# Spreading the first layer's attention gate rows with four selector products instead of transfers through memory

## The chip, the cores and the metric

The kernel runs on one NeuronCore of a Trainium2 chip. The metric is the device time of one launch in microseconds (us). Engines are named as the profile names them: PE (TensorE, matrix products), DVE (VectorE), ACT (ScalarE), POOL (GpSimd), SP (SyncE, which here only issues transfers). SBUF is the memory beside the engines, with 128 partitions; PSUM is the small memory that PE writes, eight banks of 128 x 512 float32.

## What is computed

Two token groups of 128 tokens each (t = 0, the prompt; t = 1, the sample) pass through two layers. Every layer has an attention part and a mixture-of-experts part, each with a residual that is scaled by a gate:

```python
for l in range(DEPTH):                      # 2 layers, D_MODEL = 1024
    sh, sc, g, shf, scf, gf = _modulation(cond, w_mod[l], b_mod[l])   # each 1 x 1024, per token group
    h = _adaln(x, norm_mix[l], sh, sc)      # rmsnorm(x) * (1 + scale) + shift
    o = attention(h) @ w_out                # 128 x 1024
    x = x + g * o                           # g is the same row for all 128 tokens of a group
    x = x + gf * _moe(_adaln(x, norm_ffn[l], shf, scf), w_router, ..., w_gate[l], w_up[l], w_down[l])
```

All is float32. The attention gate `g` is one row of 1024 numbers per token group. Tokens lie on the partitions, so to multiply `o` (128 tokens x 1024) by `g`, that row must stand on all 128 partitions.

## The kernel before

**Stages.** For each layer the kernel runs the input projection, the attention, the output projection, the second normalisation and the router, and then the experts. The 16 experts are taken in eight pairs; each pair streams 24 MB of weights through a ring of six slots of 2 MB (`ring`), plus some places in `work`, `gbuf`, `tmp`, `early`, `m4` and `spare` for the first pair. SP issues every weight load in a fixed order, and each load into a slot first waits for PE to have read what stood there.

**Order by hand.** During attention each engine follows a table, `FILL`. Attention has eight turns (four head batches for t = 1, then four for t = 0). In turn j, PE transposes the probabilities (`probs_transposed`, records at L799), computes the scores of turn j + 2 (L906), does what `FILL[l][(j,)]` lists, multiplies by the values (L938 or L944), and does what `FILL[l][j]` lists. The names in the table: `mod` is a quarter of the modulation product (L821), `modT` and `nextT` its transposition (L832), `wo` a half of the output projection (L868, eight products), `oT` the transposition of some outputs, `rt` router logits, `pos` token positions. ACT and DVE follow the same table for their own shares.

**Banks.** Every such PSUM result is a named job. The list `psum_jobs()` numbers them; job k is written to bank 1 + (k + 5) mod 7, and PE waits for job k - 7 to have been emptied (`bank_free`). Bank 0 is apart: it takes the modulation sums, and `keep_busy` writes there dummy 128 x 128 products (L845). When the experts of a layer begin, PE waits first for that one of the last seven jobs that lies on bank 1 (`before[0]`), since the first expert product writes banks 0 and 1; then it runs `keep_busy` (two of them in layer 0, three in layer 1) and then `gather`, whose first eight products (L1048) wait for DVE's one-hot table `picked`. The other six (`behind`) are waited for one product later.

**The gate rows.** The modulation leaves each gate as a pair of 512-wide rows in a few partitions of the tile `gates`; all its other rows but the experts' gates are zero. After DVE has added the bias (`gates_taken`), POOL runs `spread_gates(l)`: two transfers write the rows to `gate_rows` in memory (L734), then, once these have landed, two transfers read each token group's row back onto all 128 partitions of `gbuf` (L740, 512 KB each). DVE's `out_project` waits for `gate_spread[t]` and multiplies the projection's bank by `gbuf` (L1688), then adds to `x` (L1690). The experts' gates take another way already: `expert_gate_rows` multiplies `gates` by a column of the constant `selg`, repeated 128 times, so that each of four products puts one half row on all partitions of a bank (L1122), and ACT copies the banks to `gbuf` (L1418).

Of the kernel before, what the change touches and what calls it, by code (L numbers as in the profile page):

```python
# [8 lines left out]
ACT = mybir.ActivationFunctionType  # L9
# [4 lines left out]
P = 128  # L14
# [88 lines left out]
def turn(l, j):  # L103
# [10 lines left out]
        1: [("T", 0), ("mod", 0, 2, 2), ("mod", 0, 2, 3)],  # L114
        2: [("modT", 2), ("mod", 1, 0, 0), ("mod", 1, 0, 1)],
        3: [("mod", 1, 0, 2), ("oT", 1), ("mod", 1, 0, 3)],
        4: [("wo", 0, 1), ("nextT", 0)],
        5: [("wo", 1, 1)],
        (6,): [("mod", 1, 1, 0)],
        6: [("oT", 0)],  # L120
# [19 lines left out]
def banks_of(l, item):  # L140

    kind, rest = item[0], item[1:]
    if kind == "mod":
        return []
    if kind == "in":
        return [("qkv", l) + rest]
    if kind == "nextT":
        return [("modT", 1) + rest]
    if kind == "T":
        return [("T", l, rest[0], i) for i in range(2 + K_JOBS[l, rest[0]])]  # L150
    if kind == "hT":
        return [("hT", l) + rest + (h,) for h in range(2)]
    if kind == "xT":
        return [("xT", l, h) for h in range(2)]
    if kind == "hk":
        return [("hk", l, rest[0], h) for h in range(2)]
    if kind == "rt":
        return [("rt", l, rest[0])] + (banks_of(l, ("hk", 1)) if rest[0] else [])
    if kind == "pos":
        return [("pos", l), ("count", l)]  # L160
    return [(kind, l) + rest]
# [16 lines left out]
def released(l):  # L178

    order = [("mod", 0, 0, k) for k in range(4)] if l == 0 else []  # L180
    for point in points(l):
        for item in FILL[l].get(point, []):
            if item[0] == "mod":
                order.append(item)
            elif item[0] in ("in", "wo") and item[2] == 0:
# [2 lines left out]


EMPTIED_BY = {"vecT": "dve", "bT": "dve", "modT": "dve", "T": "act", "S": "act", "PT": "act",  # L190
              "O": "dve", "oT": "act", "wo": "dve", "hk": "act", "rc": "dve", "pos": "dve", "count": "dve"}


APART = ("in", 0, 4)
# [59 lines left out]
def build(nc, a):  # L254
    ctx = ExitStack()
    with ctx:
# [11 lines left out]
        hT = sb("hT", [P, DC, TT * P])  # L268
        work = sb("work", [P, 15360])
        const = sb("const", [P, NCONST])  # L270
        gates = sb("gates", [P, LAYERS, UC])
        gbuf = sb("gbuf", [P, 4, UC])
# [13 lines left out]
        rc = sb("rc", [P, NE])  # L286
# [28 lines left out]
        def K(name):  # L315
            at, n = CONST[name]
            return const[:, at:at + n]
# [45 lines left out]
        def htok(t):  # L363
# [7 lines left out]
        filled = sem("bank_filled")  # L371
        emptied = {"act": sem("bank_emptied_act"), "dve": sem("bank_emptied_dve")}
# [18 lines left out]
        gate_spread = [sem(f"gate_spread{t}") for t in range(TT)]  # L391
        gates_out = sem("gates_out")
        gate_rows = nc.dram_tensor("gate_rows", (LAYERS, TT, D), F32, kind="Internal").ap()
        copies, bias_copied = nc.dram_tensor("bias_copies", (16, 3, 64, 32), F32, kind="Internal").ap(), sem("bias_copied")
        mod_used, mod_emptied, mod_ready, gates_taken = (
            sem(n) for n in ("mod_used", "mod_emptied", "mod_ready", "gates_taken"))
# [81 lines left out]
        def fill(name):  # L478

            return number[name] + 1  # L480
# [17 lines left out]
        def emptied_by(name):  # L498

            return emptied[engine_of[name]], done_at[name]  # L500
# [5 lines left out]
        def bank_of(name):  # L506
            return bank[1 + (number[name] + SHIFT) % 7]
# [183 lines left out]
        def _(pool):  # L691
# [38 lines left out]
            def spread_gates(l):  # L730

                pool.wait_ge(gates_taken, 2 * l + 1)
                for u in range(2):
                    pool.dma_start(gate_rows[l, :, UC * u:UC * (u + 1)], gates[32 * u:32 * u + 2, l, :]).then_inc(gates_out, 16)  # L734
                if l == 1:
                    pool.wait_ge(x_ready, 8)
                    pool.wait_ge(filled, fill(("S", 1) + turn(1, BATCHES - 1) + (1,)))
                pool.wait_ge(gates_out, 32 * (l + 1))
                for t in (1, 0):
                    pool.dma_start(gbuf[:, 2 * t:2 * t + 2, :].rearrange("p u n -> p (u n)"),  # L740
                                   gate_rows[l, t].partition_broadcast(P)).then_inc(gate_spread[t], 16)

            for l in range(LAYERS):
                if l == 1:
                    power("norm", 1, 0, 1)
                    power("norm", 1, 0, 0)
                    pool.wait_ge(filled, fill(("qkv", 1, 1, 1)))
                    pool.dma_start(cache[:, 0:1024], a["cache_c_k"][0, 0].rearrange("k h d -> k (h d)")).then_inc(ld_cache[1], 16)
                    pool.dma_start(cache[:, 1024:2048], a["cache_c_v"][0, 0].rearrange("k h d -> k (h d)")).then_inc(ld_cache[1], 16)
                    pool.wait_ge(bias_copied, 48)  # L750
                    for r in range(2):
                        for r2 in range(2):
                            src = bass.AP(copies.tensor, copies.offset + (r2 - r + 1) * 64 * 32 + 15, [[31, 64], [3 * 64 * 32, 16], [1, 64]])
                            pool.dma_start(bias[64 * r:64 * r + 64, :, 64 * r2:64 * r2 + 64], src).then_inc(ld_bias, 16)
                power("qk", l, 1)
                power("qk", l, 0)

                pool.wait_ge(normed, 2 * l + 2)
                pool.wait_ge(*emptied_by(("qkv", l, IN_UNITS[l] - 1, 0)))
                if l == 0:  # L760
                    outs = [("new_a_k", 512, 128), ("new_a_v", 640, 128), ("new_b_k", 1280, 512), ("new_b_v", 1792, 512)]
                else:
                    outs = [("new_c_k", 1024, 1024), ("new_c_v", 2048, 1024)]
                for name, at, n in outs:
                    pool.dma_start(a[name], qkv[0][:, at:at + n]).then_inc(out_kv[l], 16)
                if l == 0:
                    power("sub", 0, 1)
                spread_gates(l)
                if l == 0:
                    power("sub", 0, 0)  # L770
                power("norm", l, 1, 1)
                power("norm", l, 1, 0)
# [5 lines left out]
        def _(pe):  # L778
# [82 lines left out]
            def out_project(l, u, t):  # L861
                w = ring[arrived(("out", l, u))]
                b = bank_free(("wo", l, u, t))
                pe.wait_ge(*emptied_by(("O", l, t, ORDER[l][-1])))
                if l == 0:
                    pe.wait_ge(*emptied_by(("oT", 0, t)))
                for c in range(DC):
                    ins = pe.matmul(b[:, :], oT(l, t, c), w[:, c, :], start=c == 0, stop=c == DC - 1)  # L868
                ins.then_inc(filled, 1)

            def outputs_transposed(l, t):
                pe.wait_ge(o_ready, 2 - t)
# [133 lines left out]

            def meanwhile(l, point):
                job = {"in": project, "modT": mod_transposed, "wo": out_project, "rt": logits, "hk": token_rows,
                       "oT": outputs_transposed, "hT": norm, "T": heads_transposed, "pos": positions}
                for item in FILL[l].get(point, []):  # L1010
                    if item[0] == "mod":
                        mod(*item[1:])
                    elif item[0] == "nextT":
                        mod_transposed(1, item[1])
                    elif item[0] in ("rc", "xT"):
                        {"rc": shift_logits, "xT": rows_transposed}[item[0]](l)
                    else:
                        job[item[0]](l, *item[1:])
# [207 lines left out]
        def _(act):  # L1226
# [116 lines left out]
            def probs_transposed(l, j):  # L1343
# [3 lines left out]
                for k in range(pt_jobs(l, t, b)):  # L1347
# [3 lines left out]
                                   bank_of(name)[:, 0:per * P].rearrange("p (c q) -> p c q", c=per),  # L1351
                                   ACT.Copy).then_inc(emptied["act"], 1)

            def outputs_transposed(l, t):
                act.wait_ge(filled, fill(("oT", 0, t)))
                act.activation(oT(0, t, 4, 4), bank_of(("oT", 0, t))[:, :], ACT.Copy).then_inc(emptied["act"], 1)

            def meanwhile(l, point):
                for item in FILL[l].get(point, []):
                    if item[0] == "in" and engine_of[("qkv", l) + item[1:]] == "act" or item[0] == "in" and squared_cols(l, item[1]):  # L1360
                        project(l, *item[1:])
                    elif item[0] == "mod" and item[3] == 3:
                        mod(*item[1:3])
                    elif item[0] in ("oT", "hT") or item[0] == "T" and l == 1:
                        {"oT": outputs_transposed, "hT": modulate, "T": heads_transposed}[item[0]](l, *item[1:])

            def attention(l):
                meanwhile(l, "head")
# [94 lines left out]
        def _(dve):  # L1463
# [219 lines left out]
            def out_project(l, u, t):  # L1683

                name, k, cols = ("wo", l, u, t), 2 * t + u, slice(u * UC, (u + 1) * UC)
                dve.wait_ge(gate_spread[t], 16 * (l + 1))
                dve.wait_ge(filled, fill(name))
                dve.tensor_tensor(tmp[:, k % 2, :], bank_of(name)[:, :], gbuf[:, k, :], ALU.mult).then_inc(emptied["dve"], 1)  # L1688
                dve.wait_ge(*emptied_by(name))
                dve.tensor_tensor(x[:, t, cols], x[:, t, cols], tmp[:, k % 2, :], ALU.add).then_inc(x_ready, 1)  # L1690
# [307 lines left out]
```

## Time and profile before

| | us |
|---|---|
| three runs | 1262.09, 1263.69, 1263.94 |
| median | 1263.69 |
| the profiled execution, own time | 1262.51 |
| its span | 1260.70 |
| PE busy (matmul) | 1175.7 (93%) |
| DVE busy | 280.3 (22%) |
| ACT busy | 186.8 (15%) |
| POOL busy | 56.3 (4%) |
| memory traffic | 494 MB, 392 GB/s over the span |

A busy time is the sum of the intervals in which an engine had an instruction in work. The share of the 16 DMA engines says how much of a stretch they were moving data. The profile also gives the chain of work that ended last, which goes from the last instruction back to whatever released each step. A float32 product appears in it as two records.

The main stages by time in the span: attention of layer 0 to about 190 us, its experts to 643, attention of layer 1 to about 808, its experts to the end.

### The profile page before, as it was taken

The page shows a single profiled execution, that of the slowest core. Times are in us where ns is not written, and L with a number is a line of the kernel's source. Part 1 is how long each engine was busy: PE and PEld are TensorE (multiplying, and loading weights), DVE is VectorE, ACT ScalarE, POOL GpSimd, SP SyncE. Part 2 cuts the span into 40 slices and gives each one's busy share as a digit, 9 for nine tenths or more (in the row PEclk, how much of TensorE's full clock was granted, in tenths as well). Part 3 has the DMA queues.
Part 4 walks back from the last instruction along what each step waited for, and adds up shares of the span by engine and source line. Part 5 has one row for each costly group of instructions (what it writes and reads, how often), then busy time and mean ns, then how long its engine had stood idle before and what let it go on. Part 6 is the DMA issues. An engine that isn't in the chain of part 4 may idle for free.

```text
span 1260.7 us, 13886 instructions
## 1 busy us (share of the span) xinstructions
PE 1175.7 (93%) x5521; PEld 515.2 (41%) x5521; DVE 280.3 (22%) x677; ACT 186.8 (15%) x439; POOL 56.3 (4%) x68
## 2 busy tenths in 40 slices
PE   4999999999998899898999999999999899889998
PEld 2445454443433243333344455643434334343433
DVE  1146532122010102020233353312020111102013
ACT  1224321010000000000122342210000001000010
POOL 0422000000000000000003020000000000000000
PEclk9999999999989999999999999999999999998999
DMA  9999999999999999999994678699999999999997
GB/s 374 392 378 353 414 421 428 423 400 410 426 430 427 429 427 429 428 428 429 418 389 126 221 285 347 281 405 402 371 427 431 425 432 425 432 425 432 424 425 303
DMA packets 60223, 494.07 MB, mean 392 GB/s; under 512 B 5506, under 2 KB 6674, under 8 KB 28948
## 3 DMA queue, kind: packets, MB, share of 16 engines
q1 hardware_dynamic: 57136, 485.85, 93.1%
q0 software_dynamic: 2864, 7.46, 2.0%
q8 instruction: 29, 0.48, 0.2%
q10 hardware_dynamic: 180, 0.17, 0.0%
q14 instruction: 14, 0.11, 0.0%
HBM read 490.69 MB, written 3.16 MB: 392 GB/s over the span
## 4 chain that ended last, share of the span: by engine, by line
PE 74%; DMA 20%; issue 3%; ACT 1%; DVE 1%; SPq 1%; POOL 0%; DVEq 0%
PE bank L1087 40%; DMA ring<-in_w_gate 13%; PE bank L858 12%; PE bank L868 4%; PE bank L1057 3%; DMA ring<-in_w_up 3%; PE bank L821 3%; PE bank L1048 2%; PE bank L1109 2%; DMA ring<-in_w_in_ab 2%; PE bank L799 2%; DMA ring<-in_w_down 1%; PE bank L906 1%; PE bank L1139 1%; PE bank L1122 1%
## 5 line engine op out<-in xcount | busy, mean ns | idle before, releaser
L1087 PE MATMUL bank<-ring,hT 128*64 128x512 f32 x2688 | 610.7, 610 | 60.0 <-issue 27.5
L1087 PEld LDWEIGHTS bank<-ring,hT 128*64 128x64 f32 x2688 | 204.7, 140 | 443.4 <-issue 441.9
L858 PE MATMUL bank<-ring,hT 128*128 128x512 f32 x320 | 143.0, 605 | 2.5 <-DMA ring<-in_w_in_ab 2.4
L858 PEld LDWEIGHTS bank<-ring,hT 128*128 128x128 f32 x320 | 60.9, 193 | 80.0 <-issue 77.4
L1848 DVE TENSOR_TENSOR work<-work,bank 128x512 f32<-128x512 f32 x56 | 38.5, 687 | 195.1 <-PE bank L1057 194.9
L1841 DVE TENSOR_TENSOR work<-work,bank 128x512 f32<-128x512 f32 x32 | 22.0, 688 | 229.0 <-PE bank L1087 198.0
L1048 PE MATMUL bank<-work 128*128 128x128 f32 x512 | 60.5, 276 | 0.2 <-DVE work L1822 0.2
L1048 PEld LDWEIGHTS bank<-work 128*128 128x128 f32 x512 | 58.7, 192 | 2.1 <-issue 1.6
L868 PE MATMUL bank<-ring,work 128*128 128x512 f32 x128 | 56.5, 594 | 0.3 <-DVE work L1665 0.3
L1398 ACT ACTIVATE hT<-bank 128x512 f32<-128x512 f32 x32 | 19.0, 595 | 255.2 <-PE bank L1139 255.2
L1889 DVE COPY work<-bank 128x512 f32<-128x512 f32 x14 | 9.7, 692 | 209.3 <-PE bank L1087 209.3
L1057 PE MATMUL bank<-work 128*128 128x512 f32 x112 | 51.8, 605 | 0.0
L821 PE MATMUL bank<-ring,cond 128*32 128x512 f32 x384 | 48.3, 629 | 1.5 <-DMA ring<-in_w_mod 1.0
L1109 PE MATMUL bank<-ring,hT 128*64 128x512 f32 x192 | 42.2, 593 | 0.3 <-DMA ring<-in_w_down 0.3
L1829 DVE TENSOR_TENSOR work<-work,bank 128x512 f32<-128x512 f32 x32 | 22.0, 688 | 84.7 <-ACT work L1407 84.7
L1087 PE MATMUL bank<-work,hT 128*64 128x512 f32 x152 | 39.3, 593 | 0.0
L1425 ACT ACTIVATE work<-bank 128x512 f32<-128x512 f32 x14 | 8.4, 597 | 192.9 <-PE bank L1087 192.9
L868 PEld LDWEIGHTS bank<-ring,work 128*128 128x128 f32 x128 | 23.7, 190 | 27.6 <-issue 27.6
L1411 ACT ACTIVATE work<-bank 128x256 f32<-128x256 f32 x16 | 6.1, 383 | 184.3 <-PE bank L1162 184.3
L1407 ACT ACTIVATE work<-bank 128x512 f32<-128x512 f32 x32 | 19.1, 597 | 95.2 <-PE bank L1087 95.2
L1057 PEld LDWEIGHTS bank<-work 128*128 128x128 f32 x112 | 20.1, 189 | 31.5 <-issue 31.5
L1562 DVE TENSOR_REDUCE hss<-bank 128x8 f32<-128x512 f32 (+1 forms) x16 | 10.5, 658 | 91.7 <-ACT bank L1298 91.7
(213 smaller groups left out, 718.6 us busy)
## 6 DMA issues: line engine op xcount, KB each, us to landing
ring<-in_w_gate SPq DMA_DIRECT2D x64, 2048.0 KB, 16.8
ring<-in_w_up SPq DMA_DIRECT2D x52, 2048.0 KB, 17.2
ring<-in_w_down SPq DMA_DIRECT2D x52, 2048.0 KB, 16.9
ring<-in_w_mod SPq DMA_DIRECT2D x23, 2048.0 KB, 10.2
work<-in_w_up SPq DMA_DIRECT2D x8, 2048.0 KB, 16.6
ring<-in_w_down SPq DMA_DIRECT2D x12, 1024.0 KB, 14.7
ring<-in_w_in_c SPq DMA_DIRECT2D x6, 2048.0 KB, 20.8
ring<-in_w_in_ab SPq DMA_DIRECT2D x4, 2048.0 KB, 21.6
```

The source lines that it names most:

```text
L799: ins = pe.transpose(b[:, i * P:(i + 1) * P], src, K("ident"))
L821: ins = pe.matmul(out, cond[:, 2 * k + r, :], cols, start=(k, r) == (0, 0), stop=(k, r) == (3, 1), tile_position=(0, 32 * j))
L858: ins = pe.matmul(b[:, 0:n], hT[:, c, t * P:(t + 1) * P], w[:, c, 0:n], start=c == 0, stop=c == DC - 1)
L868: ins = pe.matmul(b[:, :], oT(l, t, c), w[:, c, :], start=c == 0, stop=c == DC - 1)
L1048: ins = pe.matmul(bank[2 if first and h else h][:, c * P:(c + 1) * P], htok(t)[:, at:at + P], pick[:, t, :], start=t == 0, stop=t == 1)
L1057: pe.matmul(bank[4 + 2 * t + h][:, :], GT[:, t, :], yd[:, h * UC:(h + 1) * UC], start=True, stop=True).then_inc(m["scattered"], 1)
L1087: ins = pe.matmul(bank[banks[j]][64 * e:64 * e + 64, :], lhs[:, 4 * h + c, 64 * e:64 * e + 64], weights(e, c, j), start=(h, c) == (0, 0), ...
L1109: ins = pe.matmul(bank[banks[j]][64 * e:64 * e + 64, :], lhs[:, 4 * h + c, 64 * e:64 * e + 64], rows4[slots[e]][:, c, j * UC:(j + 1) * UC] ...
L1407: act.activation(sg[:, h * UC:(h + 1) * UC], bank[h][:, :], ACT.Sigmoid).then_inc(m["sig_done"], 1)
L1829: dve.tensor_tensor(hid[:, half], sg[:, half], bank[h][:, :], ALU.mult).then_inc(m["gate_taken"], 1)
L1841: dve.tensor_tensor(hid[:, half], hid[:, half], bank[2 + h][:, :], ALU.mult).then_inc(m["hid_done"], 1)
L1848: dve.tensor_tensor(y[:, t, cols], y[:, t, cols], bank[4 + 2 * t + h][:, :], ALU.add).then_inc(m["y_added"], 1)
```

## The change

In layer 0 the gate rows no longer go through memory. Two entries come into the table, `gs` for t = 1 in turn 4 and for t = 0 in turn 5, each between the scores and the values. For each, PE runs two products of a repeated `selg` column with `gates`, and ACT copies the two banks to `gbuf`. DVE's `out_project` waits for these copies. POOL calls `spread_gates` only in layer 1. Layer 1 keeps its transfers.

```diff
+        (4,): [("gs", 1)],
         4: [("wo", 0, 1), ("nextT", 0)],
+        (5,): [("gs", 0)],
         5: [("wo", 1, 1)],
...
+    if kind == "gs":
+        return [("gs", l, rest[0], u) for u in range(2)]
...
-                pool.wait_ge(gates_out, 32 * (l + 1))
+                pool.wait_ge(gates_out, 32)
...
-                spread_gates(l)
+                if l == 1:
+                    spread_gates(l)
...
+            def gates_spread(l, t):
+
+                pe.wait_ge(gates_taken, 2 * l + 1)
+                for u in range(2):
+                    b = bank_free(("gs", l, t, u))
+                    i = 2 * u + t
+                    pe.matmul(b[:, :], K("selg")[:, i:i + 1].to_broadcast([P, P]), gates[:, l, :], start=True, stop=True).then_inc(filled, 1)
...
+            def gates_spread(l, t):
+                for u in range(2):
+                    name = ("gs", l, t, u)
+                    act.wait_ge(filled, fill(name))
+                    act.activation(gbuf[:, 2 * t + u, :], bank_of(name)[:, :], ACT.Copy).then_inc(emptied["act"], 1)
...
-                dve.wait_ge(gate_spread[t], 16 * (l + 1))
+                dve.wait_ge(*(emptied_by(("gs", 0, t, u)) if l == 0 else (gate_spread[t], 16)))
```

PE's instructions in turn 4 of layer 0, before (scores at L906, values at L938, the output projection at L868, then the transposition of the next layer's modulation at L832):

```order
L906 MATMUL bank3<-work 128x128
L938 MATMUL bank4<-work 128x128 [waits bank_emptied_act]
L938 MATMUL bank4<-work 128x128
L868 MATMUL bank5<-ring5,work 128x512 [waits bank_emptied_dve,bank_emptied_act,dense_loaded5]
L868 MATMUL bank5<-ring5,work 128x512 x7
L832 MATMUL bank6<-const,m4 128x128 [waits bank_emptied_dve,mod_emptied]
```

and after, where the same statements have the line numbers 919, 951, 873 and 837:

```order
L919 MATMUL bank3<-work 128x128
L882 MATMUL bank4<-gates,const 128x512 [waits bank_emptied_act,gates_taken]
L882 MATMUL bank5<-gates,const 128x512 [waits bank_emptied_act]
L951 MATMUL bank6<-work 128x128 [waits bank_emptied_act,bank_emptied_dve]
L951 MATMUL bank6<-work 128x128
L873 MATMUL bank7<-ring5,work 128x512 [waits bank_emptied_dve,bank_emptied_act,dense_loaded5]
L873 MATMUL bank7<-ring5,work 128x512 x7
L837 MATMUL bank1<-const,m4 128x128 [waits bank_emptied_act,mod_emptied]
```

Two products now stand between the scores and the values, and the jobs behind them lie two banks further on. Turn 5 has the same form and moves what follows by two banks more.

Four jobs more in the list also move every later job by four banks. At the start of layer 1's experts PE has before (token counts at L1004 and L1005, three `keep_busy` products at L845, the first gathering at L1048):

```order
L1004 MATMUL bank4<-chosen,const 128x16 [waits bank_emptied_dve]
L1005 MATMUL bank4<-chosen,const 128x16
L845 MATMUL bank0<-const 128x128 [waits bank_emptied_act]
L845 MATMUL bank0<-const 128x128 x2
L1048 MATMUL bank0<-work 128x128 [waits picked1]
```

and after (L1017, L1018, L850, L1061):

```order
L1017 MATMUL bank1<-chosen,const 128x16 [waits bank_emptied_dve]
L1018 MATMUL bank1<-chosen,const 128x16
L850 MATMUL bank0<-const 128x128 [waits bank_emptied_act,bank_emptied_dve]
L850 MATMUL bank0<-const 128x128 x2
L1061 MATMUL bank0<-work 128x128 [waits picked1]
```

The token counts (job `count`) now lie on bank 1, so `before[0]` is this job, and the wait ahead of the `keep_busy` products takes in DVE's reading of it. In layer 0 the job on bank 1 is now `pos` (token positions) in place of a job of ACT.

## Rows read from the trace of the kernel before

**Rows 1.** The page: busy us, then tenths busy in 40 equal slices.

```profile
PE 1175.7 (93%) x5521; PEld 515.2 (41%) x5521; DVE 280.3 (22%) x677; ACT 186.8 (15%) x439; POOL 56.3 (4%) x68
...
DMA  9999999999999999999994678699999999999997
```

**Rows 2.** The chain that ended last, layer 0: start, length, what (us).

```profile
140.00 6.87 PE bank L868 x16
...
281.59 20.75 PE bank L1087 x96
...
330.19 21.14 DMA ring<-in_w_gate
```

**Rows 3.** Who PE waited for, 113 to 320 us (all rows): total, times, longest.

```profile
PE bank L1087 <- ACT hT L1393: 1.3, 2, 0.8
PE bank L1000 <- issue: 0.6, 1, 0.6
PE bank L799 <- ACT hT L1266: 0.5, 1, 0.5
PE bank L944 <- ACT work L1350: 0.4, 2, 0.2
```

**Rows 4.** Windows: length, busy of PE, PEld, DVE, ACT, POOL, then PEclk, DMA share, GB/s.

```profile
137.00:149.00 12.00, 11.98 (x61) 6.34 (x54) 3.17 (x11) 2.82 (x12) 0.00 (x0) 1.00 1.02 423
276.00:278.00 2.00, 2.00 (x14) 1.21 (x11) 0.69 (x1) 0.42 (x1) 0.00 (x0) 1.00 0.46 197
290.00:292.00 2.00, 2.00 (x12) 0.70 (x10) 0.00 (x0) 0.00 (x0) 0.00 (x0) 1.00 0.72 279
292.00:640.00 348.00, 318.74 (x1449) 124.94 (x1446) 51.43 (x104) 28.03 (x50) 0.00 (x0) 0.97 1.01 427
```

**Rows 5.** What SP's transfer queue waited for, 270 to 300 us.

```profile
SPq L557 <- PE bank L1087: 27.3, 3, 12.8
```

**Rows 6.** The chain: the four selector products that spread the experts' gates.

```profile
606.02 3.63 PE bank L1122 x8
```

**Rows 7.** ACT's timeline: its next instruction after turn 4's exponentials, and one gate copy.

```profile
147.59 0.38 ACT L1350 ACTIVATE work<-bank 128x256 f32<-128x256 f32 x1 [5.70 <-PE bank L799]
...
607.12 0.60 ACT L1418 ACTIVATE gbuf<-bank 128x512 f32<-128x512 f32 x1 [0.42 <-PE bank L1122]
```

**Rows 8.** Transfers of 130 to 147 us: POOL's queue, then what it carried.

```profile
q0 software_dynamic: 288, 1.05, 15.4%
gbuf<-gate_rows POOLq DMA_DIRECT2D x2, 512.0 KB, 8.1
```

**Rows 9.** DVE's first use of a gate row in layer 0.

```profile
146.98 0.69 DVE L1688 TENSOR_TENSOR tmp<-bank,gbuf 128x512 f32<-128x512 f32 x1 [6.30 <-PE bank L868]
```

**Rows 10.** Timeline at the start of layer 1's experts.

```profile
807.65 0.92 PE L845 MATMUL bank<-const 128*128 128x128 f32 x6
...
808.59 0.17 DVE L1786 TENSOR_REDUCE cnt<-bank 128x1 f32<-128x16 f32 x1
...
808.73 2.05 PE L1048 MATMUL bank<-work 128*128 128x128 f32 x16 [0.17 <-DVE work L1822]
```

**Rows 11.** Five `keep_busy` products without a wait, layer 1, PE's timeline.

```profile
802.57 1.28 PE L845 MATMUL bank<-const 128*128 128x128 f32 x10
```

**Rows 12.** Windows of layer 1, columns as in rows 4.

```profile
810.00:812.00 2.00, 1.22 (x10) 0.82 (x10) 0.62 (x4) 0.60 (x1) 0.00 (x0) 1.00 0.04 14
892.00:894.00 2.00, 2.00 (x17) 1.76 (x16) 0.69 (x1) 0.60 (x1) 0.00 (x0) 1.00 0.61 131
896.00:1240.00 344.00, 315.69 (x1442) 124.45 (x1442) 46.41 (x97) 29.11 (x52) 0.00 (x0) 0.97 1.00 425
```

**Rows 13.** The chain: 32 records of one expert product at full and at lower clock.

```profile
429.88 7.09 PE bank L1087 x32
...
469.01 8.78 PE bank L1087 x32
```

## What the change does to the time, forecast before it ran

> **What bounds the kernel now.** The page comes first: PE is busy 93% of the span, and the DMA engines show a 9 in 34 of 40 slices [rows 1]. Both look like the bound, so busy shares decide nothing here, and the stage has to be asked. The change acts on layer 0 between 118 and 165 us.
>
> The chain of waits is the second view. Through turns 4 and 5 it runs on PE from one product to the next, and it stays with it (the experts' products at 281.59 us) until 330 us, where it first passes to a weight load of the experts' loop [rows 2]. The third view says how far PE can give way: from 113 to 320 us PE waits 2.8 us in all (1.3 + 0.6 + 0.5 + 0.4), never for a transfer, and each of these waits hangs on ACT or DVE work, or on issue, that itself follows PE's own earlier results [rows 3]. In turn 4 PE is busy 11.98 of 12.00 us at full clock [rows 4]. So an instruction more on PE here has no gap to go into.
>
> That alone doesn't carry a delay to the end, since the memory also streams at 423 GB/s in the same stretch [rows 4]: if transfers set the pace, PE's delay would be swallowed. Here the windows are read for places where the DMA engines run dry. Between 276 and 278 us their share falls to 0.46, and between 290 and 292 to 0.72; from 292 to 640 us it is full, at 427 GB/s [rows 4]. What was missing in the gaps was permission: SP's queue spent 27.3 of these 30 us waiting for PE to free a ring slot [rows 5]. A DMA system that has run dry keeps no memory of work saved earlier; what it does next starts when PE lets it. So up to about 290 us layer 0 is paced by PE, and from there by transfers. The last handing over, at about 290 us, takes place as late as PE is late, and the 350 us behind it only shift. Layer 1 has the same form: the DMA engines are at 0.04 at 810 us and at 0.61 at 892 us, and full only behind that [rows 12].
>
> **The four products.** The twin of the added product runs already for the experts' gates: four products of a repeated column with `gates`, 3.63 us on the chain, 0.91 each [rows 6]. The added ones have the same operands, shapes and count. Their waits are met: `gates_taken` is raised by DVE in turn 0, and the banks they take were emptied by ACT or DVE a turn earlier. Split into two visits they cost +3.6 us on PE. As bounds: an output projection's eight products take 6.87 us, 0.86 each, with pipelining between neighbours [rows 2], which gives 3.4; one wasted gap a visit, of the size of the longest wait in rows 3 (0.8), gives 5.2. I take 3.6, since that row is the same instruction. None of it is covered, by the 11.98 of 12.00 us.
>
> The TensorE page of the Trainium skill ("TensorE: Matmul & The Clock Gate", section "Back-to-back issue gap") gives N/2.4 + 2.5 ns for an isolated matmul of N columns, 216 ns for 512. Four products would then be 0.9 us. The trace disagrees for these float32 products, at 0.91 us for one; the measurement decides.
>
> **ACT's copies.** Four copies of a 128x512 bank at 0.60 us each are 2.4 us [rows 7]. ACT does a pair behind the exponentials of turns 4 and 5. After turn 4's exponentials it idles 5.70 us until the next transposition is there [rows 7], so 1.2 us fit. In turn 5 the pair stands likewise ahead of a wait for PE's next 7 us projection. Cost 0. Were the cover gone, PE would wait for ACT to copy probabilities: up to 1.2 us a turn.
>
> **DVE's wait.** `out_project` waits for ACT's copy instead of the transfer. DVE's first use of a gate row now waits 6.30 us for the projection on PE, not for the gates [rows 9], and the copies will be done at about 143.1 us (147.59 - 5.70 + 1.2), against a projection that ends at 146.98 + 1.8 = 148.8. Behind that wait stand the residual add and the shares of turn 5; none of them moves by more than PE does. Cost 0, gain 0.
>
> **The transfers.** 1.05 MB leave POOL's queue; they took 15.4% of 16 engines over 17 us, which is 2.6 us of the whole DMA system, and landed after 8.1 us [rows 8]. The weight loads behind them may land up to 2.6 us sooner. No one waited for them up to 320 us [rows 3], and at 276 us the engines run dry whatever was saved [rows 4]. Gain 0 on the path. As a bound on the gain: 2.6 us, if transfers carried the pace after all. POOL also loses a wait for the landing of the first pair; POOL is busy 4% and its next work is asked for by DVE much later. Nothing.
>
> **The banks.** Four more jobs move every later bank by four of seven. Which job waits for which (k - 7) is the same except near the new jobs, where the job waited for is at least most of a turn old. What does change is `before[0]`, on which PE waits ahead of `keep_busy`. In layer 0 it becomes `pos`, read by DVE before PE has finished the next modulation transposition: 0. In layer 1 it becomes `count`. DVE reads the count only after its first one-hot table, from 808.59 to 808.76 us [rows 10]. PE before did its three dummy products from 807.65 us while that table was made, and began to gather at 808.73 [rows 10]. Now the dummies begin only at about 808.76 plus the 0.05 us with which PE followed DVE's table, so 808.81, and only behind them the gathering. Five such products take 1.28 us as ten records of 275 ns that overlap: (1.28 - 0.28) / 9 = 0.11 between records, 0.22 per product [rows 11]; three are 0.67 us. Gathering starts at 809.48, +0.75 us. The bounds are 0 (if the dummies slip through at once) and 0.08 + 0.92 = 1.0 (the whole interval of rows 10). The DMA engines are all but dry at 810 to 812 us [rows 12], and the next loads wait for the product behind this gathering, so these 0.75 us pass to the end too.
>
> **Sum.** 3.6 + 0.75 = 4.35 us. Against the profiled execution that is 1262.5 + 4.35 = 1266.9 (span 1260.7 to 1265.1). The profiled execution lies 1.2 under the median of the runs, and the same difference on the median gives 1263.7 + 4.35 = 1268.0.
>
> **Rivals.**
> (a) *Transfers carry the pace, and the 1.05 MB saved are worth their time.* The delay of PE in layer 0 is then swallowed by loads that have landed ahead of their use, and 2.6 us are gained; layer 1's 0.75 stays: 1263.7 - 2.6 + 0.75 = 1261.9. For it: the DMA share is full in turn 4 [rows 4], and the chain ends on weight loads in both loops. Against it: the dry gaps at 276 and 290 us. It decides if in the changed kernel no dry gap stands between 206 and 300 us; the gap now is 0.54 of 2 us, 1.1 us, at 276 to 278 and it should widen. This is the case that is not slower. The Trainium skill's "Perfetto Trace Analysis", section "Identifying the Most-Contended Engine", says to rank engines over the profile by occupancy or memory use and optimise the first; by that, with the memory close to its rate nearly throughout, less traffic should win. The trace speaks against it in this stretch.
> (b) *Part of the delay is taken back.* PE's waits of rows 3 shrink because DVE, ACT and POOL go on while PE is with the new products. At most 2 us of the 2.8 could go: 1266.0. Against it: they all hang on PE results that come later by the same amount.
> (c) *The clock falls in layer 1.* PE's idle time around 808 to 811 us rises from 0.95 us (0.17 in rows 10 and 0.78 in rows 12) to 1.7 with the dummies displaced. At the lower of the two clocks, 1.2 GHz, a stretch of 32 records took 8.78 us in place of 7.09 [rows 13], so +1.7: 1269.7. For it: the loop does lose its clock after waits of PE. Against: in rows 12 the clock stays 1.00 with 0.78 us idle in two.
> (d) *ACT or a bank delays PE in turn 4 or 5*: up to 1.2 us a turn, 1268.0 + 1.2 = 1269.2 for one.
> (e) *The displaced dummies cost nothing*: 1263.7 + 3.6 = 1267.3.
>
> **How the numbers follow.** The forecast, 1268.0, with 0.60; (a) 0.08; (b) 0.10; (c) 0.08; (d) 0.06; (e) 0.08. A measurement of this kernel can tell about 0.2%, 2.5 us, from no change. Faster by more needs under 1261.2: only (a) with a lucky spread of runs, 0.03. Within 0.2% (to 1266.2): the rest of (a), most of (b), and a tail of the forecast in runs that scatter by 1 us to either side, 0.19. Slower: 0.78. The range leaves out (a) and the far end of (c) and of (d): 1264.9 to 1270.4, where the bounds of the costs (3.4 + 0 to 5.2 + 1.0) span 1267.1 to 1269.9, and the rest is the scatter of runs and (b).
>
> **What would show it.** Right: four products of 0.9 us at two places near 140 and 150 us, no wait of PE ahead of them; PE's first record behind turn 5 late by 3.6; the dry gap that was at 276 us later by 3.6 and wider, by up to 2.6 us more; layer 1 entered 3.6 late; its dummies after DVE's count, and 0.7 to 0.8 us more by the first expert product. Wrong: weight loads of the second expert pair that start earlier relative to the span's start than before (a); a wait of PE for ACT at the values of turns 4 to 6 (d); a granted clock under 1 near 812 us (c). The forecast as a whole falls if the experts of layer 0 end less than 2 us later than before.

## The result, and the profile of the changed kernel

| | us | against before |
|---|---|---|
| before, median of 4 runs | 1263.82 (1262.09 to 1265.32) | |
| changed, median of 4 runs | 1272.12 (1271.78 to 1273.33) | ratio 1.0068, 95% interval 1.0050 to 1.0085 |
| profiled execution, before and changed | 1262.51 and 1271.78 | span 1260.7 and 1270.0 |

The changed kernel is slower by 8.3 us, where 4.35 had been forecast, and outside the forecast range of 1264.9 to 1270.4. The direction held. The place and the size of the first term, the four products, held too. The second term, 0.75 us for a wait that moved in layer 1, is where it went wrong.

The chain of waits, in order of time (start, length, what), first in layer 0; of the kernel before, beside [rows 2]:

```profile
156.15 1.85 PE bank L821 x16
...
644.50 0.88 PE bank L799 x8
```

and of the changed kernel:

```profile
138.68 1.91 PE bank L882 x4
141.04 6.87 PE bank L873 x16
149.24 1.91 PE bank L882 x4
151.60 6.87 PE bank L873 x16
158.90 1.85 PE bank L826 x16
...
647.49 0.88 PE bank L804 x8
```

The product behind turn 5 (now L826) starts at 158.90, where before it started at 156.15. But this execution ran 0.61 us ahead when it came to turn 4. PE's timeline has its scores there, before and changed:

```profile
138.58 0.71 PE L906 MATMUL bank<-work 64*128 64x128 f32 x8
137.97 0.71 PE L919 MATMUL bank<-work 64*128 64x128 f32 x8
```

That difference is scatter: in two experiments below whose code is that of the kernel before up to here, the same scores began at 137.90 and 136.98. From the scores to the product behind turn 5 it took 158.90 - 137.97 = 20.93 us, before 156.15 - 138.58 = 17.57, so the two visits cost 3.36 us. Layer 1 is entered at 647.49 in place of 644.50, which is 2.99 later, or 3.6 with the 0.61. That part is as forecast.

PE's waits from 113 to 320 us in the changed kernel are those of [rows 3] again:

```profile
PE bank L1100 <- ACT hT L1412: 1.3, 2, 0.8
PE bank L1013 <- issue: 0.6, 1, 0.6
PE bank L804 <- ACT hT L1279: 0.5, 1, 0.5
PE bank L957 <- ACT work L1363: 0.4, 2, 0.2
```

None shrank, and none was added. Now the start of layer 1's experts, PE's timeline, which answers to [rows 10]; the first line is of the kernel before, its first expert product, and the others are of the changed kernel:

```profile
811.56 7.09 PE L1087 MATMUL bank<-ring,hT 128*64 128x512 f32 x32 [0.78 <-ACT hT L1393]
...
810.41 0.37 PE L1018 MATMUL bank<-chosen,const 128*128 128x16 f32 x2
812.03 1.62 PE L850 MATMUL bank<-const 128*128 128x128 f32 x6 [1.25 <-DVE cnt L1805]
813.45 3.62 PE L1061 MATMUL bank<-work 128*128 128x128 f32 x16
817.85 8.92 PE L1100 MATMUL bank<-ring,hT 128*64 128x512 f32 x32 [0.78 <-ACT hT L1412]
```

and the windows of the same stretch (length; busy of PE, PEld, DVE, ACT, POOL; then PEclk, DMA share, GB/s), which answer to [rows 12]:

```profile
808.00:810.00 2.00, 1.61 (x13) 1.43 (x13) 1.73 (x11) 1.34 (x3) 0.00 (x0) 1.00 0.94 401
810.00:812.00 2.00, 0.78 (x7) 0.68 (x7) 1.71 (x14) 0.00 (x0) 0.00 (x0) 0.84 0.96 381
812.00:814.00 2.00, 1.97 (x9) 2.00 (x10) 1.56 (x8) 0.00 (x0) 0.00 (x0) 0.50 0.28 108
...
818.00:820.00 2.00, 2.00 (x6) 0.67 (x7) 0.00 (x0) 0.00 (x0) 0.00 (x0) 0.50 0.00 0
820.00:822.00 2.00, 2.00 (x8) 0.66 (x6) 0.00 (x0) 0.00 (x0) 0.00 (x0) 0.60 0.00 0
822.00:824.00 2.00, 2.00 (x12) 0.64 (x10) 0.00 (x0) 0.00 (x0) 0.00 (x0) 1.00 0.03 8
```

PE stands idle for 1.25 us, waiting for DVE to read the token counts (L1805). While it does, the granted clock falls to half, 1.2 GHz, and it is back only in the window of 820 to 822 us. At half clock the three dummy products, the gathering and a part of the first expert product run. The pieces are measured from PE's router logits, which stand on both chains (L966 before, L979 changed) and come 2.98 us later:

```profile
799.55 1.83 PE bank L966 x16
802.53 1.83 PE bank L979 x16
```

| | before | changed | more |
|---|---|---|---|
| start of gathering | 808.73 | 813.45 | 4.72 - 2.98 = 1.74 |
| gathering and ACT's copy | 2.83 | 4.40 | 1.57 |
| first expert product to its end | 7.09 | 8.92 | 1.83 |
| sum | | | 5.14 |

Of the first 1.74 us, 0.75 is what the forecast had, 0.24 is that PE followed DVE's reading of the counts later than forecast, and the other 0.75 is that the three dummies took 1.42 us to the start of gathering in place of 0.67. So about 1.0 us of the 5.14 is waiting, and about 4.15 us is work at the lower clock.

What follows only shifts: the first gap of issue in the experts' loop comes 8.12 us later.

```profile
935.53 2.15 issue
943.65 2.00 issue
```

The spans differ by 9.3 us since in this one execution the clock also fell once in the last pair (the chain has 8.78 us at 1210.29, before 7.09 at 1202.21). The medians differ by 8.3.

### The profile page after: what moved, and what is told of

The parts are those of the page before. It is cut to its first block, busy times and chain, and to the rows that moved or that the text cites. A ratio compares the mean times of both kernels' runs of the same rounds, so it can differ in the third digit from the quotient of the medians.

```text
span 1270.0 us, 13904 instructions
## 1 busy us (share of the span) xinstructions
PE 1179.2 (93%) x5529; PEld 518.0 (41%) x5529; DVE 280.3 (22%) x677; ACT 188.9 (15%) x443; POOL 54.2 (4%) x64
## 4 chain that ended last, share of the span: by engine, by line
PE 73%; DMA 20%; issue 3%; SPq 2%; DVE 1%; ACT 1%; POOL 0%; DVEq 0%
PE bank L1100 40%; DMA ring<-in_w_gate 10%; PE bank L863 9%; DMA ring<-in_w_up 7%; PE bank L873 4%; PE bank L1122 3%; DMA ring<-in_w_mod 3%; PE bank L1061 3%; PE bank L1070 3%; PE bank L826 3%; PE bank L804 2%; PE bank L1152 1%; PE bank L919 1%; SPq L547 1%; PE bank L1135 1%
## 5 line engine op out<-in xcount | busy, mean ns | idle before, releaser
L863 PE MATMUL bank<-ring,hT 128*128 128x512 f32 x320 | 140.3, 595 | 2.5 <-DMA ring<-in_w_in_ab 2.4
L1061 PE MATMUL bank<-work 128*128 128x128 f32 x512 | 62.1, 280 | 0.0
L1061 PEld LDWEIGHTS bank<-work 128*128 128x128 f32 x512 | 60.4, 197 | 1.7 <-issue 1.6
L826 PE MATMUL bank<-ring,cond 128*32 128x512 f32 x384 | 48.0, 625 | 3.3 <-DMA ring<-in_w_mod 2.8
L1352 ACT ACTIVATE work<-bank,nm 128x256 f32<-128x256 f32 (+1 forms) x64 | 26.0, 421 | 31.4 <-DVE nm L1657 31.4
```

Of the source, the lines that this page charges most:

```text
L826: ins = pe.matmul(out, cond[:, 2 * k + r, :], cols, start=(k, r) == (0, 0), stop=(k, r) == (3, 1), tile_position=(0, 32 * j))
L863: ins = pe.matmul(b[:, 0:n], hT[:, c, t * P:(t + 1) * P], w[:, c, 0:n], start=c == 0, stop=c == DC - 1)
L1061: ins = pe.matmul(bank[2 if first and h else h][:, c * P:(c + 1) * P], htok(t)[:, at:at + P], pick[:, t, :], start=t == 0, stop=t == 1)
L1352: ins = act.activation(PR[:, j % 2, h, 0:nk], bank_of(("S", l, t, b, e))[:, i * nk:(i + 1) * nk], ACT.Exp, bias=nm[:, j % 2, h:h + 1], sca ...
```

## The experiments

All ratios are against the kernel before on the same chip; its medians there were 1263.78 (16 runs, for the first four), 1263.47 (23 runs, for the next three) and 1263.34 us (17 runs, for the last).

### The wait alone, in the kernel before

```diff
                 pe.sem_inc(m["scattered"], 4)
+                if l == 1:
+                    pe.wait_ge(*emptied_by(("count", 1)))
                 keep_busy(3 if l else 2)
```

> The kernel before, with one wait more: in layer 1 PE waits for DVE's reading of the token counts ahead of its three dummy products, which is the order that the change brings about there through the banks. No product, transfer or bank is changed. Theory (the displaced dummies leave PE idle for about 1.2 us, its clock falls, and dummies, gathering and the first expert product run at the lower one): 1263.8 + 5.1 = about 1269, with a granted clock of 0.5 from about 809 us and the first expert product of layer 1 at 8.9 in place of 7.1 us. Rival (the forecast's own term: the dummies are only displaced): +0.75, 1264.6, clock 1.00. Rival (the excess comes from the moved banks or the new products themselves): no change, 1263.8.

Measured: 1268.53 us, ratio 1.0036 (1.0022 to 1.0051), +4.75. PE's timeline of this kernel:

```profile
806.84 0.38 PE L1005 MATMUL bank<-chosen,const 128*128 128x16 f32 x2
808.23 1.65 PE L845 MATMUL bank<-const 128*128 128x128 f32 x6 [1.01 <-DVE cnt L1788]
809.67 3.62 PE L1048 MATMUL bank<-work 128*128 128x128 f32 x16
814.07 8.81 PE L1087 MATMUL bank<-ring,hT 128*64 128x512 f32 x32 [0.78 <-ACT hT L1395]
```

It is the picture of the changed kernel, with 1.01 us of idle time, and two windows show the clock, the first of them within that idle time:

```profile
807.25:807.50 0.25, 0.00 (x0) 0.00 (x0) 0.15 (x1) 0.00 (x0) 0.00 (x0) 0.66 0.87 336
808.00:810.00 2.00, 1.77 (x8) 1.77 (x9) 1.86 (x11) 0.00 (x0) 0.00 (x0) 0.50 0.40 155
```

No product, copy, transfer or bank of this kernel differs from before. So one wait, put ahead of three dummy products, costs almost 5 us. The forecast's own term (0.75) is out, and so is the idea that the moved banks or the new products cost something of themselves: the banks matter only by the wait that they move.

### The dummies ahead of the wait, in the changed kernel

```diff
+                keep_busy(3 if l else 2)
                 pe.wait_ge(*emptied_by(before[0]))
...
                 pe.sem_inc(m["scattered"], 4)
-                keep_busy(3 if l else 2)
                 gather(0, (0,))
```

> The changed kernel with the dummy products of both layers put ahead of the wait for the job on bank 1; all else as changed. Theory: the dummies run at once, PE idles for under 1 us until the counts are read, the clock stays at 1.00, and about 5 of the 8.3 us go: 1272.1 - 5 = 1267.1, which leaves the 3.6 us of the four selector products. Rival (banks or products themselves): stays at 1272.

Measured: 1266.69 us, ratio 1.0020 (1.0010 to 1.0029), +2.9. Who PE waited for between 806 and 818 us shows what was left of the wait (total, times, longest):

```profile
PE bank L1061 <- DVE cnt L1805: 0.5, 1, 0.5
```

5.4 of the 8.3 us went, with all products and banks as changed. The wait for the counts is still there, but PE works through most of it, and the windows from 800 to 824 us all have a granted clock of 1.00.

### The wait behind the gathering, in the changed kernel

```diff
-                pe.wait_ge(*emptied_by(before[0]))
...
                 gather(0, (0,))
+                pe.wait_ge(*emptied_by(before[0]))
```

> The changed kernel with the wait for the job on bank 1 moved behind dummies and the first gathering, where only the first expert product needs it; all else as changed. Theory: the start of layer 1's experts is again as before, and only the products remain: 1263.8 + 3.6 = 1267.4, DMA engines' gap at 276 us wider. Rival (the loss of the transfers gives back what the products cost): 1263.8 or less.

Measured: 1266.64 us, ratio 1.0027 (1.0015 to 1.0040), +2.9. Its timeline has the lengths of [rows 10] and [rows 13] again:

```profile
811.18 0.91 PE L850 MATMUL bank<-const 128*128 128x128 f32 x6
812.26 2.05 PE L1061 MATMUL bank<-work 128*128 128x128 f32 x16 [0.17 <-DVE work L1841]
815.09 7.09 PE L1100 MATMUL bank<-ring,hT 128*64 128x512 f32 x32 [0.78 <-ACT hT L1412]
```

### No dummies in layer 1, in the changed kernel

```diff
-                keep_busy(3 if l else 2)
+                if l == 0:
+                    keep_busy(2)
```

> The changed kernel without the three dummy products in layer 1, wait where the change has it. It tells the dummies' own time from the clock. Theory (idle time takes the clock): PE idles some 1.3 us as in the changed kernel, the clock still falls, only the dummies' 1.6 us go from the path: about 1270.5. Rival (the dummies' displacement is the cost and the clock is chance): 1267.4, clock 1.00.

Measured: 1270.96 us, ratio 1.0054 (1.0037 to 1.0071), +7.2. PE's timeline:

```profile
814.33 3.75 PE L1061 MATMUL bank<-work 128*128 128x128 f32 x16 [1.25 <-DVE cnt L1806]
818.86 9.59 PE L1100 MATMUL bank<-ring,hT 128*64 128x512 f32 x32 [0.78 <-ACT hT L1413]
```

The three dummies are gone from the path, and only some 1.1 of the 8.3 us with them (each against its own median of the kernel before; four runs each, which spread over 1.6 and 2.5 us). The granted clock is 0.50 from 814 to 822 us, and gathering and the first expert product are again slow. So the displacement of the dummies is the small part. The large part is the clock, which is lost over the 1.25 us of idle time with or without dummies behind it.

### The bank rotation put back

```diff
-SHIFT = 5
+SHIFT = 8
...
-                            keep_busy(3, bank[5])
+                            keep_busy(3, bank[1])
```

> The changed kernel with the start of the bank rotation moved by three (and the three dummy products at the start of layer 0 on bank 1 in place of bank 5, which is free there), so that from the four new jobs on every job lies on the bank that it has in the kernel before. Layer 1 is then word for word as before; only the four products, ACT's four copies and the removed transfers of layer 0 are left. Theory: clock 1.00 at the start of layer 1's experts, 1263.8 + 3.6 = 1267.4 or the 1266.7 of the two kernels that mended the order. Rival (the mended order of waits hid a loss that lies in the banks themselves, or the reverse): not within 1 us of those.

Measured: 1266.46 us, ratio 1.0029 (1.0018 to 1.0040), +3.0. Three ways of mending the order around the wait, one of which touches no order of instructions, agree within 0.3 us (+2.9, +2.9, +3.0). What they leave is the price of the change in layer 0 alone.

### The transfers kept as dead traffic

```diff
-                if l == 1:
-                    spread_gates(l)
+                spread_gates(l)
...
-                    pool.dma_start(gbuf[:, 2 * t:2 * t + 2, :].rearrange("p u n -> p (u n)"),
+                    pool.dma_start(gbuf[:, 2 * t:2 * t + 2, :].rearrange("p u n -> p (u n)") if l else spare[:, :],
                                    gate_rows[l, t].partition_broadcast(P)).then_inc(gate_spread[t], 16)
```

(Against the kernel with the late wait; POOL waits between the two transfers, and SP waits for both ahead of its load into `spare`.)

> The changed kernel with the wait moved behind the first gathering, and with the first layer's transfers through memory put back as dead traffic: POOL writes the rows and spreads them into a tile that is free then, which SP waits for ahead of its own load there; nothing reads them. Theory (saved traffic is worth nothing where PE sets the pace): the same time as without them, 1266.7, within 0.5 us. Rival a (transfers carry the pace in part): +2.6, 1269.3.

Measured: 1266.47 us, ratio 1.0019 (1.0009 to 1.0030), +3.0. Without the traffic it was 1266.64 (the late wait, on another chip, +2.9) and 1266.46 (the rotation, on the same chip). The rival's 2.6 us more are not there, and the megabyte saved shows no worth. The windows of three places say what the transfers did. Of the kernel before:

```profile
204.00:208.00 4.00, 3.44 (x23) 2.08 (x23) 1.64 (x8) 2.15 (x3) 0.00 (x0) 1.00 0.99 406
246.00:250.00 4.00, 4.00 (x22) 1.35 (x20) 0.00 (x0) 0.06 (x1) 0.00 (x0) 1.00 0.98 385
```

of the changed kernel, where the traffic is gone:

```profile
204.00:208.00 4.00, 4.00 (x28) 2.55 (x24) 0.00 (x0) 0.03 (x1) 0.00 (x0) 1.00 0.67 187
246.00:250.00 4.00, 4.00 (x20) 1.29 (x18) 1.59 (x1) 0.60 (x1) 0.00 (x0) 1.00 0.62 201
```

of the kernel with the late wait alone, this kernel's nearest twin, where it is gone too:

```profile
204.00:208.00 4.00, 4.00 (x26) 2.16 (x23) 0.00 (x0) 0.00 (x0) 0.00 (x0) 1.00 0.82 262
246.00:250.00 4.00, 4.00 (x20) 1.29 (x18) 1.99 (x2) 0.60 (x1) 0.00 (x0) 1.00 0.71 274
280.00:284.00 4.00, 4.00 (x34) 3.68 (x33) 0.69 (x1) 1.19 (x2) 0.00 (x0) 1.00 0.54 166
```

and of this kernel, where it is back:

```profile
204.00:208.00 4.00, 4.00 (x22) 1.78 (x19) 0.00 (x0) 0.00 (x0) 0.00 (x0) 1.00 0.86 344
246.00:250.00 4.00, 4.00 (x22) 1.35 (x20) 2.46 (x2) 0.41 (x1) 0.00 (x0) 1.00 0.75 320
280.00:284.00 4.00, 4.00 (x33) 3.19 (x30) 0.69 (x1) 1.11 (x2) 0.00 (x0) 1.00 0.47 117
```

The DMA share (last but one) is the reading. Before, the engines first ran dry at 276 us. In all three kernels with the four products they run dry from 204 us on, 70 us earlier, and again at 246, while PE is busy in the whole of these windows. With the traffic back they do so nearly as much as in the twin without it. Over the whole of 190 to 330 us the share is 0.99 before, 0.96 in the changed kernel and in the twin, and 0.97 here. Transfers that stand idle in either case can't hand on a saving. Most of the new idle time is thus not the saved megabyte's; that it comes from PE freeing the ring's slots later is likely, and was not tested apart.

### The products doubled

```diff
+                    pe.matmul(b[:, :], K("selg")[:, i:i + 1].to_broadcast([P, P]), gates[:, l, :], start=True, stop=True)
                     pe.matmul(b[:, :], K("selg")[:, i:i + 1].to_broadcast([P, P]), gates[:, l, :], start=True, stop=True).then_inc(filled, 1)
```

(Against the kernel with the late wait.)

> The changed kernel with the wait moved behind the first gathering, and with each of the four selector products run twice, the second over the first in the same bank. Theory (every product in this stretch passes to the end whole): 1266.7 + 3.6 = 1270.3. Rival b (PE's waits take back part): under 1269.

Measured: 1269.70 us, ratio 1.0055 (1.0037 to 1.0073), +6.2, and 3.2 more than the two kernels of the same chip with four products. The chain of the first visit:

```profile
139.62 1.05 PE bank L882 x2
140.67 0.86 PE bank L883 x2
141.53 0.86 PE bank L882 x2
142.39 0.86 PE bank L883 x2
```

Four more products of 0.86 us are 3.44 us on PE, and 3.2 arrive at the end. The four of the change cost 3.36 on PE, and 3.0 arrive. So nearly all of each product in this stretch passes through; the scatter of the runs (2 to 3 us) doesn't resolve the remaining 0.3.

### More dummies in layer 0, in the kernel before

```diff
-                pe.wait_ge(mask_ready, l + 1)
                 b = bank_free(("pos", l))
+                if l == 0:
+                    keep_busy(2, b)
+                pe.wait_ge(mask_ready, l + 1)
```

> The kernel before with two dummy products more, in layer 0, in the bank of the token positions, in the 0.58 us that PE stands idle there waiting for DVE's router work. In the profiles of three of the experiments the granted clock fell for 3.4 us at about 195 us, at the start of layer 0's experts, as it did in layer 1 in the changed kernel; in the others it did not. Theory (idle time ahead of the experts takes the clock there too, now and then, 1.7 us a time): the profile shows no fall at 195 us and the median is 0 to 1.2 us under the kernel before, its upper runs rarer. Rival (the falls come from elsewhere, or the dummies delay the positions): the same or up to 0.5 us more.

Measured: 1263.68 us, ratio 1.0002 (0.9992 to 1.0012), no difference. That is within what the rival had. The profile shows no fall at 195 us, but neither does that of the kernel before, so it says nothing. Whether the occasional fall in layer 0 (in the second and fourth experiment and in the one with dead traffic) can be kept out this way stays open. What can be said is that the median doesn't move.

## Why the forecast was right and wrong

**What bounds the kernel, right.** PE paces layer 0 to about 290 us, and the transfers only behind that. The doubled products and the dead traffic are the two tests of it from both sides: time on PE arrives at the end, and time on the transfers doesn't.

**The four products, right.** Forecast 3.6 us on PE, measured 3.36 in the profile (1.91 us a visit on the chain, less a little overlap). At the end 2.9 to 3.0 us by three kernels, where only they are left. The Trainium skill ("TensorE: Matmul & The Clock Gate", "Back-to-back issue gap") gives 0.216 us for one isolated matmul of 512 columns, and the estimate of 0.9 us for all four that was made from it would have been too low by far: the chain has 0.86 us for one float32 product.

**ACT's copies, DVE's wait, POOL, right.** PE's waits up to 320 us are the same four rows. In the changed kernel ACT did its pair from 141.16 us, and DVE took it up at 148.01.

**The transfers, right in worth, wrong in one sign that was to show it.** Nothing was gained at the end. But the dry gap near 278 us was to widen by up to 2.6 us beyond PE's delay, and it grew little: new gaps opened at 204 and 246 us. They opened with the dead traffic too, so they can't be put down to the saved megabyte alone.

**The banks, the step that failed.** The place was right: `before[0]` becomes `count`, and PE waits for DVE ahead of its dummies. The start of the dummies was forecast at 808.81 (811.8 with the 2.98 that layer 1 is late), and came at 812.03: 0.24 us more, in which PE was slower to follow DVE than the 0.05 us taken from [rows 10]. The failing sentence is the price: three dummies at 0.22 us each, behind which gathering starts "+0.75 us". It took the durations of PE's instructions from rows at full clock and priced a wait by its length. In the profiles in which PE has work right behind the token counts, dummies first of all, the clock stays (before, and six of the experiments); in the three in which it idles there instead, it falls (changed, first and fourth experiment). With the fall the start of gathering is 1.74 us late, gathering and copy cost 1.57 more, and the first expert product 1.83: 5.14 in place of 0.75. The first experiment reproduces it with that wait alone (+4.75), and three mended kernels take it away.

**Rival (c), the right mechanism, too small and too unlikely.** It had the clock falling just here, with 0.08. It counted one product at the lower level (+1.7), since [rows 13] show such falls in a loop where they last that long. Here the low clock began within the idle time, lasted about 10 us and covered three pieces of work in a row. The reason given against it was that in [rows 12] the clock stays at 1.00 with 0.78 us idle in two. But that idle time came right behind dummies and gathering; the 1.25 us in the changed kernel came behind five small products of 16 columns (ten records) and two earlier waits. (With the 5.1 us measured here as the second term, the sum would have been 1263.7 + 3.6 + 5.1 = 1272.4.) What exactly decides was not taken apart, but the length of the gap alone does not: the windows below put the fall 0.1 and 0.6 us behind PE's last record, while 0.78 us without work left the clock at 1.00 in [rows 12].

**Rivals (a), (b), (d), (e).** (a) falls by the dead traffic, and by its own sign: dry gaps stand between 206 and 300 us in the changed kernel. (b) is at most some 0.5 us (3.36 on PE, 2.9 to 3.0 at the end), which the scatter doesn't resolve. (d) there is no wait of PE for ACT in turns 4 to 6 of the changed kernel beyond those of before. (e) the opposite happened.

**No better kernel came out of it.** All mended forms stay 3 us above the kernel before: the transfers were free in layer 0, and PE was the engine without room.

## What to carry to other kernels

Ask of each edit whether the engine that it loads is the one that sets the pace in that stage, by looking for places where the other one runs dry; a saving on the engine that waits need not reach the end. Where a list of jobs decides buffers by position, an insertion at one place changes waits far away: compare the waits of all engines over the whole program, and look at each that differs. And a wait in front of instructions that are there to keep a clock up must be priced as if they were not there, with the work behind them at the lower clock.

## What the runs showed that had not been expected

One wait of 1.0 to 1.25 us of PE, in a stretch of tiny products, brought half clock for about 10 us (0.84 in the window of 810 to 812 us, 0.50 to 820, 1.00 from 822), and equally long in the first and the fourth experiment. Falls in the experts' loop, behind waits of 2 to 3 us, mostly cost one piece of the chain 1.7 us (8.78 against 7.09 us). The work at the low level was not only the large product: the small ones grew as well, three dummies from 0.92 to 1.62 us and the gathering from 2.05 to 3.62.

The fall does not come at the end of the wait. The changed kernel's window of a quarter of a microsecond in which it lies is

```profile
811.25:811.50 0.25, 0.00 (x0) 0.00 (x0) 0.25 (x3) 0.00 (x0) 0.00 (x0) 0.69 0.98 385
```

A mean of 0.69 between 1.00 and 0.50 puts the fall at about 811.35, and PE's last record ended at 810.41 + 0.37 = 810.78, so it came some 0.6 us into the wait. In the first experiment the window of 807.25 to 807.50 has 0.66, which gives 807.33, and the last record ended at 806.84 + 0.38 = 807.22: 0.1 us into it. The end of a matrix record is modelled, so these are estimates. They say that the idle time of 1.0 to 1.25 us is the mark of the place, not a measure of what it takes to lose the clock.
